# Attention and pooling block: x^T laid out by the host instead of turned on TensorE

## The reference, cut to what matters

```python
h = x * rsqrt(mean(x*x, axis=-1) + 1e-6) * norm_w            # 512 x 2048
q, k, v, g_a, u_p, g_p = split(h @ w_in, 6, axis=-1)          # w_in: 2048 x 6144, each part 1024 wide
q, k = rms_norm per head of 64 (eps 1e-6), then partial rotation by position
a = softmax(q1 k1^T / 8) - lam * softmax(q2 k2^T / 8)         # 8 heads, two halves each
attn = rms_norm(a @ v) * 0.8 * silu(g_a)
pool = ((centred means of u_p over 2, 4, 8, 16 rows) - u_p) @ w_pool * pool_scale * silu(g_p)
out = x + concat(attn, pool) @ w_out                          # w_out: 2048 x 2048
```

## Time and profile before

| | us |
|---|---|
| median of 3 runs | 803.97 |
| the profiled execution: its own time | 802.5 |
| its span | 800.7 |
| TensorE busy | 780.2 |
| VectorE busy | 530.8 |
| ScalarE busy | 402.8 |
| GpSimd busy | 30.4 |

### The profile page before, as it was taken

The page is one execution under the profiler, slowest core; times in us unless marked ns, Lnnn a source line. Parts: engine busy times, 40 slices in busy tenths (PEclk is TensorE's granted clock), DMA queues, the critical chain, the costliest instruction groups (busy, mean ns, idle before and its releaser), DMA issues.

```text
span 800.7 us, 10143 instructions
## 1 busy us (share of the span) xinstructions
PE 780.2 (97%) x3520; PEld 645.1 (81%) x3520; DVE 530.8 (66%) x794; ACT 402.8 (50%) x654; POOL 30.4 (4%) x37
## 2 busy tenths in 40 slices
PE   3899999999999999999999999999999999999998
PEld 3688888888888888888888888888888888888886
DVE  5728766763486667626856675277666788777796
ACT  6644445543554456433646444444455466555552
POOL 1000000000000000000000000000000020233100
PEclk9999999999999999999999999999999999999999
DMA  9333622223236222232442222326222489999912
GB/s 343 90 106 105 177 78 68 74 79 105 79 110 174 61 74 79 79 105 81 138 126 75 79 79 78 105 96 167 78 79 79 157 226 295 338 255 211 199 53 105
DMA packets 67096, 101.75 MB, mean 127 GB/s; under 512 B 4865, under 2 KB 54273, under 8 KB 66561
## 3 DMA queue, kind: packets, MB, share of 16 engines
q1 hardware_dynamic: 60592, 82.52, 32.2%
q0 software_dynamic: 4608, 16.78, 10.6%
q10 hardware_dynamic: 1874, 2.18, 1.0%
HBM read 90.98 MB, written 4.19 MB: 119 GB/s over the span
## 4 chain that ended last, share of the span: by engine, by line
PE 96%; DVE 2%; ACT 1%; DMA 1%; issue 0%; DVEq 0%; ACTq 0%
PE ps L392 94%; PE ps L482 2%; DVE mixed L794 1%; DVE h_lo L784 1%; DMA mixed<-in_x 1%; ACT at_hi L570 0%; PE ps L454 0%; PE ps L384 0%; ACT h_hi L563 0%; DVE x_left L1021 0%; ACT x_rms L573 0%; DVE x_rstd L793 0%; DVEq L792 0%; ACTq L568 0%
## 5 line engine op out<-in xcount | busy, mean ns | idle before, releaser
L392 PE MATMUL ps<-h_hi,w_hi 128*128 128x512 f32 x768 | 302.2, 394 | 1.3 <-DVE h_lo L784 1.3
L392 PE MATMUL ps<-h_lo,w_hi 128*128 128x512 f32 x768 | 299.5, 390 | 0.0
L800 DVE TENSOR_TENSOR w_lo<-raw,w_hi 128x512 fp32r<-128x512 f32 x192 | 131.2, 690 | 191.2 <-ACT w_hi L585 188.6
L585 ACT CAST w_hi<-raw 128x512 fp32r<-128x512 f32 x192 | 118.8, 622 | 249.2 <-PE ps L392 248.2
L392 PE MATMUL ps<-h_hi,w_lo 128*128 128x512 f32 x768 | 205.8, 390 | 0.0
L392 PEld LDWEIGHTS ps<-h_hi,w_hi 128*128 128x128 f32 x768 | 144.3, 188 | 31.1 <-issue 1.6
L392 PEld LDWEIGHTS ps<-h_hi,w_lo 128*128 128x128 f32 x768 | 144.2, 188 | 30.5
L392 PEld LDWEIGHTS ps<-h_lo,w_hi 128*128 128x128 f32 x768 | 144.4, 188 | 29.3
L392 PE MATMUL ps<-w_hi,h_lo 128*128 128x512 f32 x224 | 87.2, 389 | 0.0
L392 PE MATMUL ps<-w_hi,h_hi 128*128 128x512 f32 x224 | 87.2, 389 | 0.0
L392 PE MATMUL ps<-w_lo,h_hi 128*128 128x512 f32 x224 | 87.2, 389 | 0.0
(11 more groups left out here) (129 smaller groups left out, 797.0 us busy)
## 6 DMA issues: line engine op xcount, KB each, us to landing
raw<-in_w_in SPq DMA_DIRECT2D x96, 512.0 KB, 3.6
tall<-in_w_out SPq DMA_DIRECT2D x16, 512.0 KB, 12.0
raw<-in_w_out POOLq DMA_DIRECT2D x12, 512.0 KB, 11.7
wide_b<-in_w_out POOLq DMA_DIRECT2D x12, 512.0 KB, 14.6
mixed<-in_x SPq DMA_DIRECT2D x4, 1024.0 KB, 8.4
tall<-in_w_out POOLq DMA_DIRECT2D x8, 512.0 KB, 14.0
kh_twice<-kh_twice SPq DMA_DIRECT2D x8, 256.0 KB, 5.2
kl_twice<-kl_twice SPq DMA_DIRECT2D x8, 256.0 KB, 5.9
```

The costliest lines, as they stand in the source:

```text
L392: last = nc.tensor.matmul(dst, lhs, rhs, start=first and i == 0, stop=final and i == len(pairs) - 1, skip_group_check=True)
L585: nc.scalar.copy(w_hi[:, h % W_SLOTS, :], raw[:, unit % RAW_SLOTS, part * 512:part * 512 + 512]).then_inc(w_hi_ready, 1)
L800: nc.vector.tensor_tensor(w_lo[:, h % W_SLOTS, :], raw[:, unit % RAW_SLOTS, part * 512:part * 512 + 512], w_hi[:, h % W_SLOTS, :].bitcast( ...
```

## The change

The host passes x a second time, transposed (`x_cols`, 2048 x 512), and norm_w with one column for each tile of 128. x^T is loaded straight into `x_turned`, in five pieces between the units of w_in. `h_hi` and `h_lo` are made from it tile by tile with norm_w as the factor, without the row's factor. TensorE transposes nothing of x. The rows of x are loaded behind (two by SP, two by ScalarE's queue), and ScalarE sums their squares at m = 5 to 8 of the first round. The row's factor is applied when V, GA, U and GP are evacuated, which moves from ScalarE to VectorE; Silu then works in place. For K and Q VectorE adds the eps row to the sums of squares before ScalarE takes Ln. The first round is written out apart from the loop on all three engines. Its core:

```diff
@@ SP
-            for t in range(ST):
-                sp.dma_start(x_rows[:, t, :], x_tiles[:, t, :]).then_inc(x_in[t], 16)
-            for unit in range(RAW_SLOTS):
-                load_in(unit, 0)
+            load_x_cols(0, 0, 2)
+            load_in(0, 0)
+            load_x_cols(1, 2, 4)
+            load_x_cols(2, 4, 8)
+            load_in(1, 0)
+            load_x_cols(3, 8, 12)
+            load_in(2, 0)
+            load_x_cols(4, 12, 16)
+            load_in(3, 0)
...
+            load_x_row(0)
+            load_x_row(1)
@@ GpSimd
-            nc.gpsimd.partition_broadcast(norm_row, norm_source, P).then_inc(norm_spread, 1)
+            pool.wait_ge(x_rstd_ready, 1)
+            for t in range(ST):
+                pool.dma_start(rstd_line[:, t * P:(t + 1) * P], x_rstd[:, t:t + 1]).then_inc(rstd_line_in, 16)
+            pool.wait_ge(rstd_line_in, 16 * ST)
+            nc.gpsimd.partition_broadcast(rstd_row[:, :], rstd_line, P).then_inc(rstd_spread, 1)
@@ TensorE (the transposes of x are gone)
+                    if first and g == K:
+                        pe.wait_ge(h_lo_ready, hk + 1)
...
+                    if first and m == 9:
+                        pe.wait_ge(eps_diag_ready, ST)
+                        pe.wait_ge(ones_set, 1)
+                        nc.tensor.matmul(ps[:, OB, :], ones_f32, eps_diag, start=True, stop=True).then_inc(eps_spread, 1)
@@ ScalarE
+            def x_high(q):
+                act.wait_ge(x_in[q if q < 2 else 1 + q // 2], 16)
+                for kk in range(2):
+                    k = 2 * q + kk
+                    nc.scalar.activation(h_hi[:, k, :], x_turned[:, k, :], ACT.Copy,
+                                         scale=nw[:, k:k + 1]).then_inc(h_hi_ready, 1)
+            def x_stats(t):
+                if t:
+                    act.wait_ge(x_squared, t)
+                act.wait_ge(x_row_in[t], 16)
                 nc.scalar.activation(at_hi[:, :, :].rearrange("p t n -> p (t n)"), x_rows[:, t, :], ACT.Square,
                                      accum_out=x_ss[:, t:t + 1]).then_inc(x_squared, 1)
+                if t == ST - 1:
+                    act.wait_ge(x_squared, ST)
+                    nc.scalar.activation(x_rms[:, :], x_ss[:, :], ACT.Sqrt, bias=eps_t[:, :],
+                                         scale=1.0 / D).then_inc(x_rms_ready, 1)
+            act.wait_ge(nw_in, 16)
+            for q in range(4):
+                x_high(q)
+                split_high(q, 0)
... in act_round
+                    if first and m <= 4:
+                        x_high(m + 3)
...
-                        rstd(wk(3 * n), ps[:, S0:S0 + 2, :], HEAD_DIM, r * 4 + n + 1)
+                        act.wait_ge(sums_raised, r * 2 + n + 1)
+                        log_exp(wk(3 * n), wk(2), HEAD_DIM, 0.0, r * 4 + n + 1)
... behind split_high(m + 3)
+                    if first and m in (1, 2):
+                        act.dma_start(x_rows[:, m + 1, :], x_tiles[:, m + 1, :]).then_inc(x_row_in[m + 1], 16)
+                    if first and 5 <= m <= 8:
+                        x_stats(m - 5)
...
-                        nc.scalar.activation(gate[:, :, :], ps[:, 2:4, :], ACT.Silu).then_inc(evacuated, 1)
+                        act.wait_ge(evacuated, r * 4 + 2 + START)
+                        nc.scalar.activation(gate[:, :, :], gate[:, :, :], ACT.Silu).then_inc(gate_ready, 1)
@@ VectorE
+            def x_low(q):
+                for kk in range(2):
+                    k = 2 * q + kk
+                    dve.wait_ge(h_hi_ready, k + 1)
+                    ins = nc.vector.scalar_tensor_tensor(
+                        out=h_lo[:, k, :], in0=x_turned[:, k, :], scalar=nw[:, k:k + 1],
+                        in1=h_hi[:, k, :].bitcast(F32), op0=ALU.mult, op1=ALU.subtract)
+                ins.then_inc(h_lo_ready, 1)
+            def scale_evac(to, g):
+                return nc.vector.tensor_tensor(to, ps[:, 2 * (g % 2):2 * (g % 2) + 2, :], twice(rstd_row), ALU.mult)
... in dve_round, ahead of the work of the same m
+                    if first and m == 9:
+                        dve.wait_ge(x_squared, ST)
+                        setup(nc.vector.tensor_scalar(x_eps[:, :], x_ss[:, :], HEAD_DIM * EPS / D,
+                                                      HEAD_DIM * EPS * EPS, ALU.mult, ALU.add))
+                        for t in range(ST):
+                            nc.vector.tensor_scalar(eps_diag[:, t * P:(t + 1) * P], ident[:, :], x_eps[:, t:t + 1],
+                                                    None, ALU.mult).then_inc(eps_diag_ready, 1)
+                        dve.wait_ge(x_rms_ready, 1)
+                        nc.vector.reciprocal(x_rstd[:, :], x_rms[:, :]).then_inc(x_rstd_ready, 1)
+                    if first and m == 10:
+                        dve.wait_ge(eps_spread, 1)
+                        nc.vector.tensor_copy(eps_row[:, :], ps[:, OB, :]).then_inc(eps_row_ready, 1)
+                    if m == 18:
+                        qk_low(0, 0)
+                    if m in (10, 18):
+                        n = int(m == 18)
+                        dve.wait_ge(squares_summed, r * 4 + n + 1)
+                        nc.vector.tensor_tensor(wk(2), ps[:, S0:S0 + 2, :], twice(eps_row), ALU.add
+                                                ).then_inc(sums_raised, 1)
... scale_evac at m = 24 (V), 33 (GA), 40 (U) and 48 (GP), each behind a wait for w_used
```

More of the change, by code:

```diff
@@ L21, with hybrid_block @@
 W_SLOTS = 4
-def hybrid_block(nc, x, norm_w, w_in, q_norm_w, k_norm_w, lq1, lk1, lq2, lk2, subln_w, w_pool,
+def hybrid_block(nc, x, x_cols, norm_w, w_in, q_norm_w, k_norm_w, lq1, lk1, lq2, lk2, subln_w, w_pool,
                  pool_scale, w_out, identity, pair_ones, rope_cos, rope_sin, inv_count, out):
@@ L178, in corner_part @@
             return corner[:, b % 2, (b // 2) * NC:(b // 2 + 1) * NC]
[L179 to L180 removed]
+        eps_diag, ones_f32 = probs[:, 0, :], gate[:, 0, 0:P]
+        rstd_line = head_out[0:1, :]
         def wk(i):
@@ L394, in products, with pe_round @@
                 return last
-            with pe.Fori(0, ROUNDS) as r:
+            def pe_round(r, first=False):
                 for m in range(HALVES):
                     g, hk = divmod(m, G_HALVES)
+                    if first and g == K:
+                        pe.wait_ge(h_lo_ready, hk + 1)
                     if hk == 0 and g == Q:
@@ L447, in _ @@
                     if m == 25:
+                        if first:
+                            pe.wait_ge(ident_in, 16)
                         pe.wait_ge(evacuated, r * 4 + 1 + START)
@@ L519, in _ @@
                         last.then_inc(pool_done, 1)
+            pe_round(0, first=True)
+            with pe.Fori(1, ROUNDS) as r:
+                pe_round(r)
             pe.wait_ge(evacuated, ROUNDS * 4 - 1 + START)
@@ L652, in act_round @@
                             nc.scalar.preload_act_table_set(LN_EXP)
+                        if first and n == 0:
+                            act.wait_ge(lam_summed, 1)
+                            nc.scalar.activation(lam_exp[:, :], lam_sum[:, :], ACT.Exp).then_inc(lam_exped, 1)
                         act.wait_ge(w_used, r * HALVES + m)
@@ L744, in act_round @@
                     if m == 48:
-                        act.wait_ge(w_used, r * HALVES + HALVES)
-                        nc.scalar.activation(wk(0), ps[:, 2:4, :], ACT.Silu).then_inc(evacuated, 1)
+                        act.wait_ge(evacuated, r * 4 + 4 + START)
+                        nc.scalar.activation(wk(0), wk(0), ACT.Silu).then_inc(pool_gate_ready, 1)
                     if last_round and 44 <= m < 47:
                         form_high(0, m - 44)
-            with act.Fori(0, ROUNDS - 1) as r:
+            act_round(0, first=True)
+            with act.Fori(1, ROUNDS - 1) as r:
                 act_round(r)
@@ L848, in chain, with qk_low @@
                     dve.wait_ge(dve_step, r * STEPS + step[0])
-                for m in range(1, HALVES + 1):
+                def qk_low(n, c):
+                    rows = slice(64 * c, 64 * c + 64)
+                    dve.wait_ge(qk_hi_ready, r * 4 + 2 * n + c + 1)
+                    nc.vector.tensor_tensor(q_low[rows] if n else kl_twice[rows, c], wk(0)[rows],
+                                            (kh_twice, q_stack)[n][rows, c].bitcast(F32), ALU.subtract
+                                            ).then_inc((k_low_ready, q_low_ready)[n], 1)
@@ L889, in dve_round @@
                         n = int(m == 22)
-                        for c in range(2):
-                            rows = slice(64 * c, 64 * c + 64)
-                            dve.wait_ge(qk_hi_ready, r * 4 + 2 * n + c + 1)
-                            nc.vector.tensor_tensor(q_low[rows] if n else kl_twice[rows, c], wk(0)[rows],
-                                                    (kh_twice, q_stack)[n][rows, c].bitcast(F32), ALU.subtract
```

(8 more changed lines are left out.)

182 lines of the change are left out of this document (74 added, 108 removed).

## The result

The kernel after has a median of 814.66 us over 4 runs (814.16 to 814.83), the kernel before 804.0: ratio 1.0135 [1.0118, 1.0153], 10.7 us slower. The forecast was 4 us slower, with a range that ended at 814.

A forecast was written before the change was run, and what follows sets the result against it. TensorE's streaming plus its waits bound the kernel. From 802.5 us: minus 3.8 (head), plus 2.2 (clock), plus 6.4 (Q's move) gave 807.3, median put at 808; range 798 to 814, the forecast's own 804 to 811.

The forecast's parts named there:

- First product near 7.5: Head: TensorE's first product starts near 7.5 us instead of 28.18, by itself 20.7 us earlier, not entered in the sum.
- Unit 4 lands at 34.6: Head loads: unit 4 of w_in lands at 34.6 us behind 12.3 MB; 31 with all at 442, 38.5 at 347.
- 17.0 from unit 4 to the sums: Head: ScalarE's and VectorE's steps from unit 4 to the sums of K's squares take 17.0 us; sums start at 51.7.
- the gain of 3.8: Head: sums of K's squares start at 51.7 instead of 55.50, gaining 3.8 us (7.4 to 0).
- The one wait of 11 us: Head, behind half 9: TensorE stands still about 11 us ahead of the matmul with the eps diagonal.
- Clock: Behind the head's gap: TensorE restarts at 1.2 GHz and loses 2.2 us, bounds 0 and 3.1.
- K's eps row costs 0, Q's 1.6 a round: VectorE's added eps row: K's is absorbed, Q's delays the first scores by 1.6 us a round, 6.4 in all.
- Evacuations by VectorE cost 0: VectorE's four evacuations a round, 1.22 us each, cost 0; 0.7 a round if the cover fails at m = 33.
- the third: Rival, head: loads slower than the sum of their rates, unit 4 at 38.5, sums at 55.6, 811.2 us; chance 0.17.
- The fourth: Rival, m = 33 or last round: VectorE late, 0.7 to 1.5 us a round on top, 811 to 814; chance 0.08.
- The second: Rival, scores: Q's move is hidden, loss 0 to 0.7 us a round, 800.9 to 803.7; chance 0.20.
- The first: Rival, head: its gain comes through, unit 4 there by half 4's end, sums 14.5 us earlier, 794.4; chance 0.10.

The follow-up runs named there:

- a1: Kernel after without the four loads of the rows of x, ScalarE squaring tiles of x^T instead (wrong sums): 802.36 us, ratio 0.9988.
- a2: Kernel after with the four lambda loads issued from GpSimd's queue at the start instead of SP's: 816.19 us, ratio 1.0163.
- b1: Kernel after with each lambda vector loaded into one partition and spread by GpSimd: 811.91 us, ratio 1.0103.
- a4: Kernel after with ScalarE's split of half 21 put ahead of Ln at m = 18: 809.25 us, ratio 1.0069.
- a3: Kernel after with the table that holds Ln and Exp loaded once right behind the root: 808.41 us, ratio 1.0058.
- d1: Kernel after with V, GA, U and GP evacuated by ScalarE as before, without the row factor there: 814.07 us, ratio 1.0132.
- b3: Kernel after with all four row loads of x on SP's queue behind units 4 and 5 of w_in: 807.27 us, ratio 1.0044.

## Why the prediction was wrong, point by point

- **First product near 7.5**: 7.51, and 7.6 to 8.8 in the experiments; the wait behind it hides the difference.
- **Unit 4 lands at 34.6**: the step that failed; it landed at 39.8, 5.2 later. Three parts, read from the stretches. The hole of four us moved 142 GB/s instead of some 390: 1.0 MB or 2.5 us. Outside it the stream made 381, the weighted mean of my rates was 392: 0.9. And 12.9 MB had moved when it landed instead of my 12.3: 1.7. SP issued unit 4 at 24.31 and units 5 and 6 at 24.98 and 25.62, so these ran beside it, and I had counted neither; that the 0.6 MB are theirs was not followed. I had listed the lambda loads by their bytes, which say nothing of their cost. The rate I got by a mean over known stretches; the bound that I named, 38.5 with all at 347, did not hold it either. That the rows cost a head's gain is shown by a1, the hole's cause by a2 and b1. The Trainium skill ("DMA: Bandwidth & Descriptors", "Where 436 GB/s comes from") has loads from HBM bound near 358 GB/s for a core; the estimate by it, 37.4 for unit 4, was nearer than mine. The trace agrees with it for the rows (361 in a1) but not for a ceiling: 3 to 20 us went at 375 and single stretches at 400 and more.
- **17.0 from unit 4 to the sums**: 16.1. So the gain of 3.8 became a loss of 0.4. The one wait of 11 us that I put at half 9 was two, 8.3 at half 8 and 6.2 at the diagonal.
- **Clock**: a loss of 2.2 behind the gap. It was 0.9 in the sums; the slow matmuls ahead of them (half 8 and the diagonal) lie in the head, in part hidden. Another 2.7 stood where I had not looked, behind the long wait at round 0's scores.
- **K's eps row costs 0, Q's 1.6 a round**: rounds 1 to 3 had 1.35, 1.32 and 1.24, and a4 shows the mechanism. Round 0 had 3.37. I had entered the root's table load and not the ones after it: K's and Q's Exp both stood behind one. a3 takes them away and 2.3 of the 3.4 go. The trace of before showed one load only, ahead of all Ln and Exp.
- **Evacuations by VectorE cost 0**: right in the rounds within 0.2, and 0.6 at the end (d1).
- **Rivals**: the third (loads slower than the sum of their rates) had the right effect and was even too mild; half of the delay came from the lambda loads and not from the two queues that it named. The fourth (VectorE late elsewhere, 0.7 to 1.5 a round) is refuted by d1. The second, a hidden move of Q, needed a shift under 0.3; it was never near. The first would have needed no rows: a1 has its sums at 44.3, and even there the waits at Q and the diagonal leave it even with before.

In the sum: 3.8 + 0.4 at the head, 2.7 + 0.9 − 2.2 for the clock, 7.3 − 6.4 for Q and 0.5 at the end are 7.0 of the 7.3 by which the profiled execution (814.62) missed 807.3.

## What to carry to other kernels

When an edit frees TensorE at the head but keeps the bytes, write down the transfer that the next wait hangs on and what is queued ahead of it, and look at the number and size of pieces besides the bytes. Statistics over the contraction dimension can be had from the transposed operand by a matmul with ones, which removes the second load and the way back across partitions (19.5 us here). Where an edit puts a root among Ln and Exp, follow the table loads until the old table is back.

## What the runs showed of the hardware

- 512 pieces of 256 bytes, 128 of them from each of four addresses, slowed a stream of some 390 GB/s for two to seven us, from SP's and from GpSimd's queue alike; in the kernel after that cost 2.5 us. Their landing varied by 4.5 us over four kernels with the same loads, one profiled execution each, and unit 4 with it; no run shows whether the build or the execution decides it. The Trainium skill ("DMA: Bandwidth & Descriptors", "Why small descriptors are slow (HBM only)") gives 27% overhead for pieces of 256 bytes. The trace has more than that: on SP's queue the rate fell to a quarter with a DMA share of 0.32, so the engines were idle; on GpSimd's (a2) it fell to a half with a share of 0.96 to 1.00, so they were busy. What they waited for, or were busy with, no run tells.
- Ln and Exp got a table load each in round 0, though one table holds both: preloaded, they followed each other (a3). The Trainium skill ("ScalarE: Activation LUTs", "Table sets: the hidden batching unit") counts one load for Ln and then Exp; here that held only where the kernel asked for the joint table itself.
- What a wait at round 0's scores costs in clock varied. From the scores to the transposes, 3.63 us before, it took 6.36 behind a wait of 3.37, 5.11 behind 3.31 (d1), 5.28 behind 3.18 (b1), 5.36 behind 3.03 (a2), 5.37 behind 2.77 (b3), but 3.77 behind 3.34 (a1), and 3.77 behind 1.70 (a4). So up to 2.6 us hang on something beside the length of the wait, which no run here tells.
- In the first microseconds the granted clock reads 1.00 (3 to 20 us above) while the first matmuls follow each other at 0.43 us, from 7.51 to 13.2. There the durations tell the clock and the row does not.
